# Two attentions in a diffusion backbone: smaller work units, one unit of distance between producer and consumer, two kv heads side by side in the array

## What is computed

```python
# layer 0: 8 query heads, 2 kv heads (4 query heads each), head width 64, a sink logit per head
s_loc = jnp.where(valid[None, :, None, None], s_loc, NEG)      # |q - k| <= 128 among the 256 x tokens
p = jax.nn.softmax(jnp.concatenate([s_ctx, s_loc, s_sink], axis=-1), axis=-1)
o = p_ctx @ vc + p_loc @ vw          # context queries: 256 context keys and the sink only
# layer 1, x queries only, 8 differential heads of 2 x 64:
p = jax.nn.softmax(s, axis=-1)
w = p[:, :, 0] - lam * p[:, :, 1]
return jnp.einsum('bhqk,bkhe->bqhe', w.astype(v.dtype), v)
# followed by rmsnorm(o, subln_g) per head and @ w_out
```

## Time and profile before

| what | us |
|---|---|
| median of 3 runs (1974.87 to 1977.59) | 1975.62 |
| the profiled execution, whole | 1977.56 |
| its span, first to last instruction | 1975.8 |
| first attention, first score to first output matmul | 136.77 to 240.62 |
| second attention, the same | 803.76 to 909.49 |
| from the experts' first product to the end | 969.5 to 1975.8 |

### The profile page before, as it was taken

One profiled execution on the slowest core, in us unless ns is written; L12 is line 12 of the kernel. 1 busy time (PEld: TensorE's weight loads), 2 busy tenths in 40 slices (PEclk: granted clock), 3 DMA queues, 4 the chain that ended last, 5 costly groups with the idle time before them and its releaser, 6 DMA issues. The chain is left out here.

```text
span 1975.8 us, 35831 instructions
## 1 busy us (share of the span) xinstructions
PE 1820.3 (92%) x16214; PEld 1069.0 (54%) x16214; DVE 475.0 (24%) x762; ACT 386.9 (20%) x662; POOL 34.8 (2%) x71
## 2 busy tenths in 40 slices
PE   5999789999999889865799999999999999999995
PEld 2743478888888768544535345353443534435342
DVE  3313445222233663454310100101001010010103
ACT  3223433222232432342100000100001000010001
POOL 1000100000000000000000000000000000000000
PEclk8998899999999999987699999999999999999997
DMA  9255462332324232347599999999999999999970
GB/s 372 96 171 171 144 187 72 99 100 93 107 86 138 69 109 84 129 150 271 228 339 367 369 363 375 327 364 373 368 361 335 364 371 361 368 334 365 369 294 24
DMA packets 141160, 477.43 MB, mean 242 GB/s; under 512 B 11168, under 2 KB 35096, under 8 KB 122576
## 3 DMA queue, kind: packets, MB, share of 16 engines
q1 hardware_dynamic: 137344, 467.64, 64.5%
q0 software_dynamic: 3664, 7.48, 1.2%
HBM read 473.96 MB, written 1.13 MB: 240 GB/s over the span
## 5 line engine op out<-in xcount | busy, mean ns | idle before, releaser
L950 PE MATMUL ps<-w_hi,h_t 128*128 128x512 f32 (+1 forms) x960 | 298.2, 391 | 18.9 <-DVE h_t L1532 7.2
L950 PE MATMUL ps<-w_moe,h_te 128*32 128x256 f32 (+1 forms) x3520 | 296.6, 493 | 16.4 <-DVE residual L1876 16.4
L950 PE MATMUL ps<-h_t,w_hi 128*128 128x512 f32 (+1 forms) x768 | 222.5, 374 | 5.0 <-DVE h_t L1532 5.0
L950 PEld LDWEIGHTS ps<-w_moe,h_te 128*32 128x32 f32 x3520 | 113.2, 111 | 193.3 <-issue 138.9
L950 PE MATMUL ps<-w_raw,h_te 128*32 128x256 f32 (+2 forms) x3648 | 216.8, 396 | 0.0
L1479 DVE TENSOR_TENSOR w_lo<-w_raw,w_hi 128x2048 fp32r<-128x2048 f32 x58 | 132.9, 2292 | 349.0 <-ACT w_hi L619 348.5
L950 PEld LDWEIGHTS ps<-w_hi,h_t 128*128 128x128 f32 x960 | 182.6, 193 | 59.7 <-issue 8.3
L950 PE MATMUL ps<-w_lo,h_t 128*128 128x512 f32 (+1 forms) x480 | 186.9, 389 | 0.0
L1875 DVE TENSOR_TENSOR residual<-silu_g,ps 128x512 f32<-128x512 f32 (+1 forms) x32 | 19.8, 618 | 650.7 <-ACT silu_g L894 650.7
L619 ACT ACTIVATE w_hi<-w_raw 128x2048 fp32r<-128x2048 f32 x58 | 110.8, 1914 | 327.9 <-PE ps L950 319.4
L950 PEld LDWEIGHTS ps<-w_raw,h_te 128*32 128x32 f32 x3648 | 112.2, 110 | 100.9 <-issue 61.5
(11 more groups left out here) (233 smaller groups left out, 1213.6 us busy)
## 6 DMA issues: line engine op xcount, KB each, us to landing
w_moe<-in_expert_in_w_dram SPq DMA_DIRECT2D x110, 1024.0 KB, 6.2
w_raw<-in_expert_out_w_dram SPq DMA_DIRECT2D x62, 1024.0 KB, 7.1
w_raw<-in_expert_in_w_dram SPq DMA_DIRECT2D x50, 1024.0 KB, 7.7
w_raw<-in_ada_w_dram SPq DMA_DIRECT2D x48, 1024.0 KB, 5.0
w_moe<-in_expert_out_w_dram SPq DMA_DIRECT2D x34, 1024.0 KB, 7.0
work<-in_expert_in_w_dram SPq DMA_DIRECT2D x32, 1024.0 KB, 7.2
w_raw<-in_expert_in_w_dram SPq DMA_DIRECT2D x64, 512.0 KB, 4.8
w_raw<-in_ffn_in_w_dram SPq DMA_DIRECT2D x44, 512.0 KB, 4.9
```

The lines of the kernel that those rows point to most:

```text
L950: return pe.matmul(out_, l, r, start=first, stop=last, skip_group_check=True)
```

## The change

The groups become 16 units in each attention. In the first one a unit is (query tile, j) and holds one query head of either kv head: its two score matmuls stand next to each other and use rows 0-63 and 64-127 of the array, and its value matmuls alternate between columns 0-63 and 64-127. In the second a unit is one head. A unit uses two of the four score banks and half of the probability buffer, by turns. TensorE's stream per unit is: `scores(u + 2)`, transposes of u, values of u - 1, one ada block; the maxima, scaling and output steps of the other engines are put in the matching order. In the second attention the scaling of the first part (L1750) is gone: VectorE adds the second part with a factor of -lam times the ratio of the sums, and ScalarE applies the reciprocal sum when it copies and squares the output. All three first blocks of `B_DOUT` are split inside the loop (units 13, 14, 15), the two of `B_MIXOUT` in units 13 and 15. `ada_rows(3)` and `ada_rows(5)` come after the loop, before the last output; `sub_norm(0)` in unit 11.

```diff
-        def scores0(g):
+        def scores0(u):
...
+            t, j, p = u // 4, u % 4, 2 * (u % 2)
+            if u >= 2:
+                pe.wait_ge(exps, u - 1)
+            for kv in range(2):
+                q_ = QT0[HD * kv:HD * kv + HD, j, t * P:(t + 1) * P]
                 if t < XT:
-                    mm(ps[:, j, :], q_, KT0[p0:p0 + HD, :], True, False)
+                    mm(ps[:, p + kv, :], q_, KT0[HD * kv:HD * kv + HD, :], True, False)
...
+        for u in range(U0):
+            if u < U0 - 2:
+                pe.wait_ge(exps, u + 1)
+                scores0(u + 2)
+            pe.wait_ge(prob_scaled, u + 1)
...
+            if u:
+                values0(u - 1)
+            ada(2 * DK + u)
+        values0(U0 - 1)
...
+            if u < U0 - 2:
+                maxima0(u + 2)
+            if u < U0 - 1:
+                scale0(u + 1)
+            if u:
+                output0(u - 1)
+            if u == 8:
                 ada_rows(2)
-            if g == 6:
-                ada_rows(3)
+            if u in (13, 15):
+                lo_upto(B_MIXOUT + (u - 11) // 2)
+        ada_rows(3)
+        output0(U0 - 1)
...
+        def combine1(u):
+            p, r = 2 * (u % 2), 2 * (u % 4)
+            dve.wait_ge(exps, U0 + u + 1)
+            link(dve.reciprocal(RL[:, r:r + 2], SUMS[:, p:p + 2]))
+            link(dve.tensor_scalar(NRL[:, p:p + 1], RL[:, r + 1:r + 2], LAM[:, 0:1], SUMS[:, p:p + 1],
+                                   ALU.mult, ALU.mult))
+            dve.scalar_tensor_tensor(out=P1[:, p, :], in0=P1[:, p + 1, :], scalar=NRL[:, p:p + 1], in1=P1[:, p, :],
+                                     op0=ALU.mult, op1=ALU.add).then_inc(prob_scaled, 1)
...
+            if u >= 13:
+                lo_upto(B_DOUT + u - 12)
```

More of the change, by code:

```diff
@@ L814, in _, with exps1 @@
         act.activation(LAM[:, 2:4], LAM[:, 0:2], ACT.Exp).then_inc(lam_exp, 1)
[L815 to L819, removed]
+        def exps1(u):
+            p = 2 * (u % 2)
+            act.wait_ge(negmax, U0 + u + 1)
+            if u >= 2:
+                act.wait_ge(p_tr, T0 + u - 1)
+            for j in range(p, p + 2):
                 ins = act.activation(P1[:, j, :], ps[:, j, :], ACT.Exp, bias=NEGM[:, j:j + 1], scale=SCALE,
@@ new lines, in scores0, with values0 @@
+            if t < XT:
+                far = P * (1 - t)
+                for kv in range(2):
+                    ins = mm(ps[:, p + kv, far:far + P], ID[:], TRI[:, P * t:P * t + P], False, True)
+            ins.then_inc(scores, 1)
+        def values0(u):
+            t, nc_ = u // 4, 4 if u < 8 else 2
+            pe.wait_ge(z_lo, 8 + u)
+            pe.wait_ge(pt_even, u + 1)
+            pe.wait_ge(pt_odd, u + 1)
+            for c_ in range(nc_):
+                tk = c_ if t < XT else c_ + 2
+                for kv in range(2):
+                    ins = mm(ps[HD * kv:HD * kv + HD, 6, 0:P], V0[:, tk, HD * kv:HD * kv + HD],
+                             PTU[:, u % 2, kv, c_, :], c_ == 0, c_ == nc_ - 1)
+            ins.then_inc(pv_done, 1)
@@ L1132, in _ @@
-        pe.wait_ge(z_lo, 16)
+        for u in range(U0):
+            nc_ = 4 if u < 8 else 2
+            if u < U0 - 2:
+                pe.wait_ge(exps, u + 1)
+                scores0(u + 2)
+            pe.wait_ge(prob_scaled, u + 1)
+            for kv in range(2):
+                if u:
+                    pe.wait_ge(pt_even if kv == 0 else pt_odd, u)
+                for c_ in range(nc_):
+                    ins = pe.transpose(ps[:, 4 + kv, c_ * P:(c_ + 1) * P],
+                                       PR0[:, 2 * (u % 2) + kv, c_ * P:(c_ + 1) * P], ID[:])
+                ins.then_inc(p_tr, 1)
+            if u:
+                values0(u - 1)
+            ada(2 * DK + u)
@@ new lines, in scale0 @@
+        def scale0(u):
+            p, nk = 2 * (u % 2), 512 if u < 8 else 256
+            dve.wait_ge(exps, u + 1)
+            link(dve.tensor_tensor(RL[:, p:p + 2], SUMS[:, p:p + 2], ES[:, p:p + 2], ALU.add))
+            link(dve.reciprocal(RL[:, p:p + 2], RL[:, p:p + 2]))
+            for kv in range(2):
+                ins = dve.tensor_scalar(PR0[:, p + kv, 0:nk], PR0[:, p + kv, 0:nk], RL[:, p + kv:p + kv + 1], None,
+                                        ALU.mult)
+            ins.then_inc(prob_scaled, 1)
```

305 lines of the change are left out of this document (133 added, 172 removed).

## The result

The kernel after takes 1918.45 us (median of four runs, 1917.27 to 1922.03); the kernel before, in runs beside it, 1975.24. The ratio is 0.9716 with a 95% interval of 0.9697 to 0.9734: 2.8% faster, 56.8 us.

A forecast was written before the change was run, and what follows sets the result against it. TensorE was taken to bound the first attention and the experts, waiting the second attention. Savings of 25.8 and 19.7 us, together 45.5 from 1977.56, gave 1932.1 us; 8-in-10 range 1923 to 1948.

The forecast's parts named there:

- first: start to T(0): First attention, first scores to first transposes: scores, maxima, small steps, exponentials and scaling take 8.1 us.
- T(0) to T(8): First eight units: 34 us plus 5 for the clock in the first attention, 30.7 us in the second.
- T(8) to T(15): Later units with their waits at unit 8 and near the end: 23.6 us in the first attention, 30.2 in the second.
- second: start to T(0): Second attention, start to first transposes: scores, maxima behind VectorE's other work, exponentials and combination take 7.5 us.
- T(15) to the transposes of the output: End of second attention: third block's load, ScalarE's wait with the last output behind, ada copy and norm, 11.6 us.
- I add 5: Start of first attention: slow clock costs 5 us, as for about 10 us of work at half speed; bounds 0 and 10.
- The experts' loads shift with the stage: Expert stage after both attentions: its loads move along with the earlier finish; no saving added to the sum.
- Rival 5: Better: the clock stays up at both attentions' starts and the split waits hide, 1922 to 1926 us; 10%.
- 1: Rival in the first attention: column halves of the values run one after the other, 11 us more, 1942 us; 10%.
- 4: Rival in the first attention: row halves don't overlap, scores stay at 2.9 us, values unpacked too, 1952 us; 4%.
- Rival 2: Clock stays at 0.50 through both attentions, about 2003 us, 4%; milder form 1940 to 1947 us, 12%.
- Rival 3: Attention ends grow: block lands in 10 us, or queued waits add 3 us in each attention, 1938 to 1942 us; 10%.

The follow-up runs named there:

- e_after_again: The kernel after, unchanged, run again for a second profile; 1921.21 us, ratio 0.9722 to the kernel before.
- g_fill: Kernel after with splits, ada rows and norm moved at both attentions' ends, and ada blocks filling idle time at both starts; 1899.47 us.
- e_scores_apart: Kernel after, but in the first attention each head's 512-key score matmul is followed by its own mask product; 1933.97 us.

## Why the prediction was right, and too small

The profiled execution came out 12.7 us below the 1932.1 of the sum, and the trace says where (T(u) is the start of the transposes of unit u, as in the prediction):

| term | forecast | after | e_after_again |
|---|---|---|---|
| first: start to T(0) | 8.1 | 6.8 | 7.6 |
| T(0) to T(8) | 34 + 5 for the clock | 32.9 | 33.8 |
| T(8) to T(15) | 23.6 | 23.5 | 23.5 |
| T(15) to the projection | 6.8 + 0.5 | 7.5 | 7.5 |
| second: start to T(0) | 7.5 | 8.5 | 8.5 |
| T(0) to T(8) | 30.7 | 28.9 | 28.7 |
| T(8) to T(15) | 30.2 | 29.8 | 31.4 |
| T(15) to the transposes of the output | 11.6 | 11.4 | 11.5 |
| from there to the projection | 5 + 1.0 | 5.2 | 5.1 |

- **The prices of the units were right**: 4.8 and 2.8 us forecast, 4.60 and 2.80 measured; 3.5 and 3.54 in the second attention. Rows of packed matmuls elsewhere in the trace of before carried them.
- **The waits that would be left were right**, nearly all within 0.5 us: 1.5 at unit 8 (1.30) and 3.6 ahead of T(15) (3.26) in the first attention; 1.9 at unit 8 (1.81), 1.3 around the norm (0.70) and 4.3 ahead of T(15) (3.84) in the second, and 11.6 from there to the output's transposes (11.4). ScalarE's wait on the third block, which the text named as a part of those 11.6, is 0.28 us.
- **The step that failed is "I add 5"**: the clock at the start of the first attention. It was read from one profile of before, where 8 us at 0.50 stood in a busy TensorE. It was taken as 10 us of work at half speed; in the profile after the clock did not fall there at all and the cost was 0, in the second one it was 3.4 us at the low clock (PEclk 0.86 over 12 us), and the stage was 1.6 us longer. With it goes the start, 8.1 for 6.8 to 7.6. Those two are 6.3 of the 12.7 us; 3.2 are behind the second attention, 2.1 in it.
- **Slips in the working**: 7 x 2.8 is 19.6 and not 19.4, 7 x 3.5 is 24.5 and not 24.7, and 8 x 3.5 - 1.0 + 3.4 is 30.4 and not 30.7. Together they are 0.3 us and change nothing.
- **The base was a draw as well.** The same code gave 103.85 and 100.90 us for the first attention. By the second profiles its saving is 28.6 us, not 33.2, against my 25.8; the second's is 19.8 to 21.9 against 19.7.
- **"The experts' loads shift with the stage", priced at nothing**: what is behind the second attention took 1063.1 instead of 1066.3. Over all profiles it is 1061.2 to 1067.4 with the new second attention (eleven, mean 1063.4) and 1064.8 to 1067.1 with the old one (three, mean 1066.1). The ranges overlap, no experiment took it apart, and its cause stays open. The text also said that the expert stage keeps its 1006.3 us: from the experts' first product to the end it is 1004.0 after (913.58 to 1917.6), 1005.7 and 1004.0 in the second profiles of before and after. So 2.3 of the 3.2 us are there.
- **The range was too narrow on the good side.** Rival 5 ended at 1922 and asked for both starts and the split waits. The split waits were not hidden, the second start was slow (0.79), and yet the time is lower, since I had taken 1977.56 as the base where the median was 2 us less and had left the stages behind no share.
- **The rivals**: 1 and 4 fell by the unit's rows (1.02 us for 16 entries of values, 1.06 for a pair of scores) and by the two experiments that set the halves apart. Rival 2 fell too: the clock stayed at 1.00 from 148 to 164 us with 1.0 us of transposes in each 4.6. The Trainium skill's page "TensorE: Matmul & The Clock Gate", section "Part 4: PE-mode transpose", had given that rival its ground; nothing here shows the transposes pulling the clock down. Rival 3 didn't come: the ends took 3.84 and 11.4 us for 4.3 and 11.6.

What I had weighed least carries half of the result. The text priced the distance only in the second attention, as waiting that goes. The runs show that both need it: without it the short units lose 27 us against e_after_again with outputs first in their turn, and 51 with the order of the kernel after. That is not a gain of 27 us over the waits of the kernel before, whose long groups hid the copies in the first attention (0.25 to 0.34 us of waiting in a group); it is what short units would cost there. The packing is the gain of the first attention. From the rows, four heads cost 5.79 - 3.22 us less for scores and masks and 3.57 - 2.04 less for values with 512 keys, and 1.92 - 1.26 and 1.83 - 1.18 less with 256. Over four groups of each kind that makes 21.6 of the 28.6 to 33.2 us. No run has long groups with distance, or short units without packing, so the share of the smaller unit by itself is not shown.

## What to carry to other kernels

Make work units small only together with distance: a unit of time between the transposes and the products that use them is worth 27 us here, over both attentions. The two packings are worth 21.6 us by the rows, all in the first; the orders that took them away cost only some 10 and 4 us, since the column halves still overlapped in part. Where a product reuses a bank, put the step that frees the bank first in its engine's turn, or give it a unit of distance too. Fill a gap at a stage's start with work that waits for nothing, and read a clock dip from several profiles before pricing it: the same code differed by 3 us in one stage. These prices are of this kernel with its fp32 products.

## What the hardware showed that was not expected

- Two matmuls of 64 rows and 512 columns in different row halves take 1.06 us, one alone 1.05. A 128x128 product between them undoes it (2.85 instead of 1.61 us for the pair and its masks).
- Column halves overlap across two matmuls of one half followed by two of the other (0.59 us, as when alternating) and half-way across four and four (1.51 between 1.02 and the 2.0 of no overlap).
- TensorE's clock at a stage's start differs between profiles of the same code (0.64 and 1.00 over 136 to 148 us). The Trainium skill's page "TensorE: Matmul & The Clock Gate", section "Part 1: The HAM clock gate (the "warmup" mystery)", calls the ramp at a kernel's start variable from run to run; the traces here show such differences in the middle of a kernel, between 136 and 164 us. At the start of the second attention, around a gap of 4.54 us, it fell in all ten profiles that have this gap; in the first, after a gap of 1.74 us, in six profiles of nine; in g_fill, with gaps of 0.74 and 0.86 us, not at all. The gap alone does not decide it: TensorE had stood idle for only 0.90 us before the stage when the clock fell at about 139 us in the profile before, and for 0.50 us in e_scores_apart.
